# Loading x already transposed, with the vectors and S5 tables laid out beforehand, in a two-block transformer kernel

## What is computed

```python
def first_block(x, norm_mix_g, w_in, ...):
    h = rmsnorm(x, norm_mix_g)          # x * rsqrt(mean(x*x)+eps) * gain
    proj = h @ w_in                     # 2048 -> 4096 columns
    u, qkv = proj[..., :1024], proj[..., 1024:]
    y_pool = rmsnorm(pool_mixer(u, pool_w, pool_scale), pool_out_norm_g)
    y_attn = rmsnorm(dilated_attention(q, k, v), attn_out_norm_g)
    x = x + concat(y_pool, y_attn) @ w_out
    x = x + square(relu(rmsnorm(x, norm_mlp_g) @ w_up)) @ w_down
    return rmsnorm(x, norm_final_g)
```

## Time and profile before

| | |
|---|---|
| median of 3 runs | 2811.44 us (2805.94 to 2814.49) |
| the profiled execution's own time | 2814.81 us |
| its span in the trace | 2813.0 us |
| granted PE clock, mean over the span | 0.981 of full speed |
| busy: PE, PEld | 2704.0 us (96%), 2397.3 us (85%) |
| busy: DVE, ACT, POOL | 1878.4 us (67%), 1268.7 us (45%), 269.4 us (10%) |
| DMA | 589.92 MB, mean 210 GB/s |

### The profile page before, as it was taken

How to read it: one execution, slowest core, us unless ns; L and a number is a source line. 1 busy time by engine, 2 the same in 40 slices (tenths; PEclk the granted TensorE clock), 3 DMA queues, 4 the chain that set the end, 5 groups by cost and what they waited for, 6 DMA issues and landing times.

```text
span 2813.0 us, 41511 instructions
## 1 busy us (share of the span) xinstructions
PE 2704.0 (96%) x15803; PEld 2397.3 (85%) x15803; DVE 1878.4 (67%) x2204; ACT 1268.7 (45%) x1573; POOL 269.4 (10%) x317
## 2 busy tenths in 40 slices
PE   5999999999999998999999999999979999999998
PEld 5998778888888887999999899999868888888886
DVE  3686767776777777766576888767655555555556
ACT  4344454444444445455455444444454444444443
POOL 1013000000000000043003755000000000000000
PEclk8999999999999998999999999999989999999999
DMA  8875777877778776665544344578846666666664
GB/s 202 268 236 171 247 258 249 267 258 255 248 247 276 252 255 202 200 188 181 166 164 158 128 156 150 183 263 271 296 126 204 193 188 192 189 189 189 192 189 142
DMA packets 292487, 589.92 MB, mean 210 GB/s; under 512 B 25794, under 2 KB 26356, under 8 KB 291588
## 3 DMA queue, kind: packets, MB, share of 16 engines
q1 hardware_dynamic: 290212, 576.39, 63.7%
q0 software_dynamic: 2144, 11.71, 1.7%
HBM read 583.02 MB, written 5.00 MB: 209 GB/s over the span
## 4 chain that ended last, share of the span: by engine, by line
PE 82%; DVE 9%; ACT 3%; DMA 3%; issue 3%; SPq 0%; DVEq 0%; ACTq 0%
PE ps L469 80%; DVE w_lo L1585 2%; DVE arena L1580 2%; DMA w_raw<-in_w_in 2%; ACT w_hi L1045 1%; DMA w_raw<-in_w_out 1%; PE ps L546 1%; DVE arena L2151 1%; ACT arena L1070 1%; PE ps L536 0%; DVE x L1595 0%; DMA w_raw<-in_w_gate 0%; ACT arena L1088 0%; DVE x L2222 0%; SPq L419 0%
## 5 line engine op out<-in xcount | busy, mean ns | idle before, releaser
L1585 DVE TENSOR_TENSOR w_lo<-w_raw,w_hi 128x1024 fp32r<-128x1024 f32 x904 | 1118.7, 1240 | 869.7 <-ACT w_hi L1045 866.3
L1045 ACT ACTIVATE w_hi<-w_raw 128x1024 fp32r<-128x1024 f32 x904 | 951.5, 1054 | 1422.2 <-PE ps L469 1284.2
L469 PE MATMUL ps<-hop_hi_part,w_hi 128*128 128x256 f32 x2256 | 654.5, 290 | 17.2 <-DVE w_lo L1585 15.3
L469 PE MATMUL ps<-hop_lo_part,w_hi 128*128 128x256 f32 x2256 | 643.6, 285 | 0.0
L469 PE MATMUL ps<-hop_hi_part,w_lo 128*128 128x256 f32 x2256 | 643.4, 285 | 0.0
L469 PE MATMUL ps<-w_hi,hop_hi_part 128*128 128x512 f32 x1472 | 578.8, 393 | 4.4 <-DVE hop_lo_part L1638 1.8
L469 PE MATMUL ps<-w_hi,hop_lo_part 128*128 128x512 f32 x1472 | 574.8, 390 | 0.0
L469 PE MATMUL ps<-w_lo,hop_hi_part 128*128 128x512 f32 x1472 | 574.5, 390 | 0.0
L469 PEld LDWEIGHTS ps<-hop_hi_part,w_hi 128*128 128x128 f32 x2256 | 438.2, 194 | 22.4 <-DVE w_lo L1585 13.0
L469 PEld LDWEIGHTS ps<-hop_lo_part,w_hi 128*128 128x128 f32 x2256 | 438.6, 194 | 0.7 <-issue 0.2
L469 PEld LDWEIGHTS ps<-hop_hi_part,w_lo 128*128 128x128 f32 x2256 | 438.1, 194 | 0.0
(11 more groups left out here) (302 smaller groups left out, 1861.5 us busy)
## 6 DMA issues: line engine op xcount, KB each, us to landing
arena<-in_ada_w SPq DMA_DIRECT2D x256, 384.0 KB, 4.6
w_raw<-in_ffn_w_in SPq DMA_DIRECT2D x176, 512.0 KB, 3.7
w_raw<-in_w_in SPq DMA_DIRECT2D x152, 512.0 KB, 3.9
w_raw<-in_w_up SPq DMA_DIRECT2D x128, 512.0 KB, 4.1
w_raw<-in_w_down SPq DMA_DIRECT2D x128, 512.0 KB, 4.4
w_raw<-in_w_gate SPq DMA_DIRECT2D x128, 512.0 KB, 3.7
w_raw<-in_ffn_w_out SPq DMA_DIRECT2D x88, 512.0 KB, 3.6
w_raw<-in_w_out SPq DMA_DIRECT2D x64, 512.0 KB, 5.7
```

The lines of the kernel that those rows point to most:

```text
L469: return nc.tensor.matmul(o, w, r, start=start, stop=stop, skip_group_check=True)
L1045: return nc.scalar.activation(o, i, ACT.Copy, scale=scale)
L1585: V.tensor_tensor(w_lo[:, j % LEAD, :, 0:cols], w_raw[:, j % RAW, :, 0:cols], w_hi[:, j % LEAD, :, 0:cols].bitcast(F32), ALU.subtract).the ...
```

## The change

x comes in already transposed (`x_by_dim`, 128 partitions by 16 tiles by 256 tokens) in four pieces of 2, 2, 4 and 8 tiles, into `arena` tiles 16 to 31, alternating with the first four weight units. All norm and other vectors come as one array of 128x400 laid out on the host, one DMA into `vecs`; the S5 tables come as one array read in five pieces of whole rows. The PE transposes of x, the gain and the vectors go, and ACT's copies of them. x by token, still needed for the residual and the sums of squares, and the constants are loaded by SP behind weight units 5 to 9. POOL's small loads, nine now, wait until DVE has split 12 units. The jobs on the sums of squares, the inverse root and the bias table move to later units, `scaled_chunk(0)` from step 7 to step 14, `ADA_FIRST` to units 9 to 26.

```diff
-N_SMALL = 10
+N_SMALL = 9
-ADA_FIRST = [6 + k * 18 // 15 for k in range(KT)]
+ADA_FIRST = [9 + k * 17 // 15 for k in range(KT)]
+X_PIECES = ((0, 2), (2, 4), (4, 8), (8, 16))
 # SP
-        load_x(0)
-        sp.dma_start(const[:, 0:P], consts[:, 0:P]).then_inc(sem["ident_in"], 16)
-        load_vector("norm_mix_g", sem["ident_in"])
-        for i in range(1, 4):
-            load_x(i)
+            k0, k1 = X_PIECES[i]
+            sp.dma_start(T(XT + k0, k1 - k0), x_by_dim[:, k0:k1]).then_inc(x_in[i], 16)
+        def load_tokens(c):
+            sp.dma_start(x_tok[:, :, part(c)],
+                         a["x"][0][:, part(c)].rearrange("(t p) d -> p t d", p=P)).then_inc(sem["tokens_in"], 16)
+        load_x(0)
+        sp.dma_start(vecs[:], columns).then_inc(sem["vec_in"], 16)
         for q in range(RAW):
             load(0, q, w_in[q, :, :, IN_ORDER[0] * COLS:(IN_ORDER[0] + 1) * COLS], cond=False)
-        for name in VEC:
-            if name != "norm_mix_g":
-                load_vector(name, sem["vec_in"])
-        sp.dma_start(const[:, P:], consts[:, P:]).then_inc(sem["const_in"], 16)
+            if q < 3:
+                load_x(q + 1)
...
+                if g == 0 and 5 <= j < 9:
+                    load_tokens(j - 5)
+                if (g, j) == (0, 9):
+                    sp.dma_start(const[:], consts).then_inc(sem["const_in"], 16)
 # PE
-        pe.wait_ge(sem["ident_in"], 32)
-        nc.tensor.transpose(PS[0][:, 0:KT], span(48, 0, P)[0:KT, :], ident[0:KT, 0:KT]).then_inc(sem["gain_turned"], 1)
-        for b in range(KT // 2):
...
-            if u == 7:
+            if u == 14:
                 pe.wait_ge(sem["inverse_ready"], 1)
...
-            if u == 9:
+            if u == 17:
                 pe.wait_ge(drained[0], H_IN + 2)
 # ACT
+        copy(tok_guess[:, 0:1], ones[:, 0:1])
+        act.wait_ge(sem["vec_in"], 16)
         for b in range(KT // 2):
...
-                m = token_square(SUM_X, b // 2, x_tok, 16 + 4 * (b // 2))
-            if b >= 4:
-                split(0, b - 4, first=True)
+            for k in range(2 * b, 2 * b + 2):
+                m = copy(hop_hi[:, k], T(XT + k), scale=vec("norm_mix_g", k))
+            m.then_inc(sem["hop_hi"], 2)
+            if b < LEAD:
+                split(0, b, first=True)
...
+            if 7 <= u < 11:
+                if u == 7:
+                    act.wait_ge(sem["tokens_in"], 64)
+                m = token_square(SUM_X, u - 7, x_tok, (0, 4, 12, 38)[u - 7])
 # DVE
-            if j % UA == UA - 1 and j // UA < 7:
+            if j == 14:
+                dve.wait_ge(sem["inv_psum"], 1)
+                then(V.tensor_copy(inv0, PS[4][:, 0:S]))
+                scaled_chunk(0)
+            if j == 15:
+                bias_rows()
+            if j % UA == UA - 1 and 0 < j // UA < 7:
                 scaled_chunk(j // UA)
 # POOL
         pool.wait_ge(sem["cleared"], 1)
+        pool.wait_ge(sem["lo_ready"], 12)
...
-        for o, name in ((s5b[0], "s5_b_re_2"), (s5b[1], "s5_b_im_2")):
-            small(o[:], a[name][0].rearrange("(i h) s c -> (h s) i c", h=2))
+        for o in (*s5b, *s5c):
+            small(flat(o[:]), s5_in[:, at:at + 256])
```

More of the change, by code:

```diff
@@ L134, with vector_columns, s5_columns @@
 VEC_ROWS = [sum(k for _, k in rows) for rows in VEC_GROUPS]
-N_VEC_DMAS = sum(len(rows) for rows in VEC_GROUPS) - 1
+VEC_COLS = (len(VEC_GROUPS) - 1) * P + VEC_ROWS[-1]
+X_PIECES = ((0, 2), (2, 4), (4, 8), (8, 16))
+S5_COLS = 16 + 2 * 16 * S5_CH + 2 * 4 * S5_STATE
+def vector_columns(inputs):
+    v = np.zeros((P, VEC_COLS), np.float32)
+    for name, (g, r, k) in VEC.items():
+        v[:, g * P + r:g * P + r + k] = np.reshape(inputs[name], (k, P)).T
+    return v
+def s5_columns(inputs):
+    b = [np.reshape(inputs[n], (16, 2, S5_STATE, S5_CH)).transpose(1, 2, 0, 3).reshape(P, 16 * S5_CH)
+         for n in ("s5_b_re_2", "s5_b_im_2")]
+    c = [np.reshape(inputs[n], (4, 8, S5_CH, S5_STATE)).transpose(1, 2, 0, 3).reshape(P, 4 * S5_STATE)
+         for n in ("s5_c_re_2", "s5_c_im_2")]
+    steps = np.repeat(np.reshape(inputs["s5_log_dt_2"], (16, 2)).T, S5_STATE, axis=0)
+    return np.ascontiguousarray(np.concatenate(b + c + [steps], axis=1))
 def shape_constants():
@@ L173, in shape_constants @@
     return np.concatenate([c[n] for n in CONST], axis=1)
[L176 removed]
+SEMS = """const_in gain_turned gain_ready vec_in tokens_in small_in x_turned cs_ready lam_sums lam_exps
 bias_rows_ready bias_psum bias_copied bias_in hi_ready lo_ready unit_done drained0 drained1 sq_ready sum_ready
@@ L217, in two_blocks @@
     gains = sb("gains", [P, P])
-    gain0, gain5, gain6, gain7, gain8 = (gains[:, i * KT:(i + 1) * KT] for i in range(5))
+    gain5, gain6, gain7, gain8 = (gains[:, i * KT:(i + 1) * KT] for i in range(1, 5))
     gain_rows = arena[:, 71, 0:P]
@@ L1664, in by_token @@
             return ap.unsqueeze(1).to_broadcast([P, tiles, S])
-        dve.wait_ge(sem["gain_turned"], 1)
-        V.tensor_copy(gain0, PS[0][:, 0:KT]).then_inc(sem["gain_ready"], 1)
-        dve.wait_ge(sem["gain_ready"], 1)
         for b in range(KT // 2):
             dve.wait_ge(sem["hop_hi"], 2 * (b + 1))
-            for k in range(2):
-                m = stt(hop_lo[:, 2 * b + k], PS[4 + b % 4][:, k * S:(k + 1) * S], gain0[:, 2 * b + k:2 * b + k + 1],
-                        hop_hi[:, 2 * b + k].bitcast(F32), ALU.mult, ALU.subtract)
+            for k in range(2 * b, 2 * b + 2):
+                m = stt(hop_lo[:, k], T(XT + k), vec("norm_mix_g", k), hop_hi[:, k].bitcast(F32), ALU.mult, ALU.subtract)
             m.then_inc(sem["hop_ready"], 2)
-            if b >= 4:
-                split(0, b - 4)
+            if b < LEAD:
+                split(0, b)
         def bias_rows():
@@ L1755, in _ @@
             split(R_IN, j + LEAD)
-            if j == 6:
-                bias_rows()
-            if j == 4:
+            if j == 11:
                 token_variance(1, SUM_X, sem["tok_sums"], 1)
-            if j == 5:
+            if j == 12:
                 token_inverse(1, SUM_X)
+                dve.wait_ge(sem["const_in"], 16)
                 for t in range(TT):
@@ L2344, in _ @@
             small(gate_b[:], a["ml_gate_b_2"][0].rearrange("w h -> h w"))
[L2345 to L2348, removed]
         small(wa2, a["gla_wa2_2"][0])
-        for o, name in ((s5b[0], "s5_b_re_2"), (s5b[1], "s5_b_im_2")):
-            small(o[:], a[name][0].rearrange("(i h) s c -> (h s) i c", h=2))
-        for o, name in ((s5c[0], "s5_c_re_2"), (s5c[1], "s5_c_im_2")):
-            small(o[:], a[name][0].rearrange("(t g) c s -> (g c) t s", t=4))
+        at = 0
+        for o in (*s5b, *s5c):
+            small(flat(o[:]), s5_in[:, at:at + 256])
+            at += 256
+        small(s5v[:, 15, :], s5_in[:, at:at + 16])
         pool.wait_ge(sem["bias_copied"], 1)
```

75 lines of the change are left out of this document (26 added, 49 removed).

## The result

The changed kernel ran at 2785.82 us (median of 4 runs, 2781.05 to 2787.41), beside 2810.2 us for the kernel before on the same chip: a ratio of 0.991 (95% interval 0.989 to 0.9931). It is faster by 24.4 us. The forecast was 2782.5, 3.3 us too low. The profiled execution took 2787.41 us (span 2785.6, before 2814.81 and 2813.0); PE is busy 2693.3 us of it (97%), the mean granted clock is 0.988.

What follows compares the result with a forecast made beforehand. Bound by PE's matmul stream (82% of the chain) after a start waiting for the first weight unit. Terms -30.4 - 0.5 + 0.5 + 0 + 0.9 + 0.4 = -29.1 gave 2782.5 us; range 2777 to 2790, 8 in 10 2776 to 2796.

Steps and rivals of the forecast that it cites:

- (1): Start: first weight unit lands at 6.0 us, PE begins at 8.5 instead of 38.88: -30.4 us (bounds -31.2 and -26.9).
- (6): Modulation at unit 27: last ada addition moves from step 24 to 26, +0.4 us (0 to 1.5).
- (4): Units 5 to 16: load queue at 335 GB/s keeps up with PE, 0 us (bounds 0 and +5.7).
- rival A: Queue carries only 280 to 300 GB/s, PE waits in units 3 to 16: about 2790 us; chance 0.18.
- (2): PE work removed: the four transposes at unit 2 leave the chain, -0.5 us.
- (3): Units 3 and 4: unit 3 lands at 15.6 us and PE waits +0.5 us before unit 4.
- my sign of 320: Forecast's sign in the profile: windows from 5 to 55 us at DMA share near 1 and 320 GB/s or more.
- (5): `scaled_chunk(0)` late, after unit 14: banks free after PE is ready for unit 16, +0.9 us (0 to 1.5).
- (7): Sums of squares, `bias_rows`, `lam_sums`, moved bias matmuls and POOL's later work and nine loads: counted at nothing.
- B: POOL's small loads land as slowly as before, bias matmuls after unit 17 wait: 8.8 us, 2791; chance 0.05.
- C: Queue as slow as in the first 40 us: whole gain lost at 202 GB/s, 2822 us at 180; chance 0.03.
- D: Something behind unit 27, say POOL's chain, sets the end, which does not move: 2811 us; chance 0.04.

Runs made afterwards that it cites:

- the jobs first: Changed kernel with ACT's job of step 12 and DVE's jobs of steps 12 and 14 ahead of the split; 2781.66 us (0.9905), run again 2780.36 (0.9894).
- the kernel with both together: Changed kernel with jobs of steps 12 and 14 ahead of the split and first modulation one unit later; 2779.58 us (0.9883), run again 2781.38 (0.9887).

## Why the prediction was right, and where its steps were off

For the profiled execution the forecast was -29.1 us, and -27.4 was measured. At unit 32, where the forecast put its whole sum, it was -23.4. The steps missed by 5.7 us, and 3.5 of this came back later by something that was not in the forecast. That part was luck: the number is better than its working.

In the range, the worst case of "about -24" is not the sum of the bounds of (1) to (6), which is -16.6; with (4) left to rival A it is -22.3.

**(1) The start, -30.4, was right: -30.1.** The unit landed at 6.3 us (forecast 6.0) and PE began at 8.82 (8.5). The 2 us at half clock after it are in both traces. **(2), the four transposes, -0.5, was right.** **(3) Unit 3, +0.5, was right:** it landed at 16.08 us (15.6), and PE waited 0.5.

**(4) The queue in units 5 to 16, at 0, is the step that failed,** and not by the bound that I gave it. It was argued by rate: 11.4 MB by 37.5 us at 335 GB/s, with waits below 326. The rate was there: 317 to 415 GB/s from 5 to 55 us, 359 on average, though two windows of 317 lie a little below my sign of 320. What I left out is how long one load takes in a full queue. SP may issue unit j only when DVE has split unit j-4, so a load has the lead of the splits to land in; at a share of 1 it took 10.4 us (42.09 to 52.5, unit 16) where I had a median of 4.1. ACT waited 14.5 us for weights in nine waits from 20 to 70 us. PE's matmuls on the weights did not feel it in these units; `w_hi` and `w_lo` are four units ahead. The inverse and chunk 0 did: they stand behind a split on ACT and DVE and inherit its lateness. So (4) cost +1.6 at the inverse, which I had nowhere, and **(5)** +2.4 instead of +0.9: I had ended the split of unit 18 at 2.4 us after unit 14 by the spacing of the earlier trace rows, which holds only while the weights are in time. It ended at 60.31 us, 5.5 after unit 14: the weights of unit 16 landed at 52.5, then came ACT's table load of 1.28 us and its part of the inverse root, which stood in no term, and from 55.12 us on DVE had its jobs and splits without a gap. That the order turns lateness into a stop is shown by the second execution of the jobs first, with 15.0 us of lateness and 0.9 us of stops. The size varies from one execution to the next: 3.7, 2.4 and 1.1 us of stops, with 14.5, 15.2 and 6.2 us of lateness, in three traces of the same program up to unit 26.

**(6) The modulation, +0.4, cost +2.4.** The wait was close, 0.7 us. What I left out is that it is followed by 3.4 us at half clock (105.1 to 108.5), for 1.6 us; I had given such a price to the stops in (4) and not to this one. **(7)** held: nothing of it was seen on PE. POOL's nine loads took 0.50 to 0.67 us each to issue, beside DVE's splits, and landed in about 6 us.

**The cause of the old start** was named as the small pieces, the tables and `log_dt` together. Of the part that these loads make, it is `log_dt` above all, 16.5 us against 2.7 for the tables, though the table with the last landing of the earlier trace rows pointed to these: they stood behind `log_dt` in the same queue.

**The rivals.** A's sign, ACT waiting for `w_raw` by DMA in units 4 to 16, did come, but its mechanism did not: the queue carried 317 GB/s and more, 359 on average, where A had 280 to 300, and the price was about half of A's. B did not happen: `bias_rows` started at 64.06 us without a wait. C's rate of 202 GB/s was nowhere in these units. D was wrong: the offset did not shrink behind unit 32. Between units 26 and 32 it did shrink, from -25.8 to -23.4, which was one of my signs of being wrong; that is the modulation of (6) with its price, not another thing that sets the end.

**Still open** is what sets the half-clock stretches behind unit 66. Behind 195 us they fill 79 us of the trace of before and 64.6 of that of the changed kernel, and the two executions of the jobs first gain there as well (from -29.4 at unit 66 to -35.7 in one execution, from -29.9 to -34.7 in the other), the kernel with both together less (-30.1 to -33.4, and -30.8 to -31.9). No experiment ties this to the change.

## What to carry to other kernels

Look at what share of the DMA engines a small load takes, not at its bytes: 8 KB in pieces of 4 bytes, the same 16 words for each of 64 partitions, held all engines for 14 us, and together with the tables cost most of the gain again when moved into the busy part of the kernel. Lay such a table out beforehand; moving it was no remedy here.

When prefetches fill the queue, a load's landing time is the one that it has in the full queue, and every job that stands behind a prefetch's split on an in-order engine is late with it. Put the jobs that PE waits for ahead of the split: here this gave 5.7 us (1.0 to 7.6) for no other cost, part of it by fewer stretches at half clock.

## What the hardware showed that I had not expected

The elements of `log_dt`, 4 bytes each and the same words for 64 partitions, cost 112 ns each (64 in a packet of 7.2 us on average; 121 ns and 7.7 us in the kernel with the S5 loads later), and such packets stopped the other queue to 0 to 2 GB/s at a share of 1.01 to 0.64, so a high DMA share alone does not mean that anything moves. Two of the 32 packets, the first on record, took 0.08 us, so the cost is not fixed by the form of a packet alone.

A stop of 0.7 us before the one-column matmuls of the modulation was followed by a stretch at half clock in four of five traces (from 105.1, 104.4, 104.0 and 99.8 us; none in the fifth, the second execution of the jobs first). The stops of 1.5 and 2.2 us before the matmuls at 56 and 62 us of the changed kernel had none directly behind them (the next began at 70.9, behind the bias matmuls); in its second execution a stretch began at 60.1 us, just as the stop of 2.2 us ended. Four stops of 0.8 to 1.4 us before unit 16 in other kernels had none directly behind them. The window around the first of the four, in the changed kernel:

```profile
105.00:110.00 5.00, 5.00 (x30) 4.90 (x30) 0.88 (x6) 1.13 (x2) 0.00 (x0) 0.66 0.61 196
```

PE is busy all through, with 30 matmuls where a window at full clock has 44. So a short stop can cost more than its length, and not in every execution.
